# Feed-forward gate and up products as seven block products in place of eight

## The chip, the cores and the metric

The kernel runs on one core of one Trainium2 chip. The metric is the device time of one execution in microseconds, the median of several. The program is one forward pass of a small model on 512 tokens, written engine by engine with semaphores: every engine (PE for matrix products, ACT and DVE for elementwise work, POOL, and SP for issuing transfers) has its own instruction list, which it runs in order.

## The reference, cut to what matters

Two of the layers end in a SwiGLU feed-forward on the normed rows (D = 1024, D_FF = 2816, 512 tokens, fp32):

```
def swiglu(h, w_gu, w_down):
    u = h @ w_gu
    g, v = u[..., :D_FF], u[..., D_FF:]
    return (jax.nn.silu(g) * v) @ w_down

h = h + swiglu(rmsnorm(h, norm_g[layer, 1]), ffn_w_gu[layer], ffn_w_down[layer])
```

All other parts (recurrent mixer, compressed attention, retention and window attention, experts) are not touched.

## The kernel before, in words

Activations lie transposed: features on the 128 partitions, 512 tokens along the row. fp32 products are made of three fp32r products: each operand is split in a rounded high part and the rest (weights: ACT copies a_raw to a_hi, DVE subtracts to a_lo; `high_a`, `low_a`, for the down weights `high_b`, `low_b`), and `three` (L650 to L654) does high x high, high x low, low x high. hn_hi and hn_lo hold the normed input without its 1/rms, which DVE multiplies in later from rn.

A feed-forward stage has 22 panels of w_a (FF_TILES), two to a pair, so 11 pairs. A panel holds 128 gate columns and 128 up columns for all eight blocks of 128 input features (KT = 8). `linear` makes gate and up tiles of 128 x 512 in two PSUM banks (8 blocks x 3 matmuls each), DVE scales the gate (L2407), ACT takes Silu (L1701), DVE scales again (L2409) and multiplies with up (L2412) to hid, ACT and DVE split it (L1703, L2414). After two panels `down` (48 matmuls into banks 4 to 7, in two halves) multiplies with two panels of w_b, and DVE adds each bank to h (`add_y`, L2236). `ffn` runs the first pair apart (`linear_first` follows the input blocks as they come; `sums`, `root_wide` and `inverse_wide` make rn meanwhile) and the other ten in a loop. SP loads w_a panels (1024 KB) and w_b panels (512 KB) with `load_a` and `load_b`, each when the split of the panel two before is done. POOL only helps with the sum of squares. Banks and buffers alternate with the panel's parity; semaphores a_ready, b_ready, tile_ready, tile_free, hid_ready, y_ready and y_free order the engines.

## Time and profile before

| | us |
|---|---|
| runs | 2140.57, 2140.81, 2142.0; median 2140.81 |
| profiled execution, span from first to last instruction | 2139.6 |
| PE busy, share of the span | 2097.5, 98% |
| DVE, ACT, POOL busy | 1267.3, 836.2, 270.8 |
| the two feed-forward stages, first to last matmul, about | 246 to 606 and 1037 to 1398 |

The profiled execution's own time is not recorded beside its span; the median of the runs lies 1.2 us above the span. A row of the timeline gives start and duration of an instruction. Matmuls are pipelined, so their spacing is the difference of two starts, not the duration.

### The profile page before, as it was taken

How to read it: one execution, taken by the hardware profiler on the slowest of the kernel's cores; microseconds unless marked ns; L12 is line 12 of the kernel's file. 1: busy time of each engine (PE TensorE's matmuls, PEld its weight loads, DVE VectorE, ACT ScalarE, POOL GpSimd, SP SyncE). 2: the span in 40 equal slices, each digit the busy share in tenths (PEclk: the TensorE clock that was granted, in tenths of full speed). 3: DMA queues.
4: the chain of work that ended last, by engine and by line, in shares of the span. 5: the costliest groups of instructions: out<-in, count | busy, mean ns of one | idle time of the engine just before them, and what ended most of it. 6: DMA issues, size and time to landing. Idle time of an engine off the chain costs nothing.

```text
span 2139.6 us, 27223 instructions
## 1 busy us (share of the span) xinstructions
PE 2097.5 (98%) x10474; PEld 1579.8 (74%) x10474; DVE 1267.3 (59%) x1704; ACT 836.2 (39%) x1258; POOL 270.8 (13%) x234
## 2 busy tenths in 40 slices
PE   8999999999999999999999999999999999999998
PEld 6787788888878877888888888877778884333346
DVE  7887855554587678875655555488775454000038
ACT  6556522222253444774422222264542232222143
POOL 1334200000010064000100000020000023222220
PEclk9999999999999999999999999999999999999999
DMA  5322322223214352122322222212122158999961
GB/s 202 125 94 74 118 92 105 88 88 117 79 64 147 130 172 79 31 46 90 131 91 99 104 88 88 98 61 78 60 99 98 62 239 321 418 408 401 391 238 60
DMA packets 62622, 298.13 MB, mean 139 GB/s; under 512 B 14080, under 2 KB 14464, under 8 KB 34582
## 3 DMA queue, kind: packets, MB, share of 16 engines
q1 hardware_dynamic: 42560, 261.60, 32.0%
q0 software_dynamic: 19552, 34.55, 5.3%
q8 instruction: 63, 1.03, 0.2%
q10 hardware_dynamic: 416, 0.70, 0.1%
q14 instruction: 31, 0.25, 0.0%
HBM read 326.37 MB, written 22.48 MB: 163 GB/s over the span
## 4 chain that ended last, share of the span: by engine, by line
PE 80%; DVE 8%; DMA 5%; ACT 3%; issue 2%; POOL 1%; POOLq 0%; ACTq 0%; DVEq 0%
PE psum L652 21%; PE psum L654 21%; PE psum L653 21%; PE psum L1413 5%; PE psum L1437 3%; DMA panel<-w_m 3%; PE psum L1102 2%; PE psum L1077 1%; DVE a_lo L2137 1%; DMA over_panel<-w_m,over_row 1%; ACT a_hi L1520 1%; DVE xc L2294 1%; DVE hs L2248 1%; ACT hn_hi L1547 0%; PE psum L1235 0%
## 5 line engine op out<-in xcount | busy, mean ns | idle before, releaser
L652 PE MATMUL psum<-hn_hi,a_hi 128*128 128x512 f32 (+1 forms) x1592 | 628.2, 395 | 1.9 <-DVE a_lo L2126 0.9
L654 PE MATMUL psum<-hn_hi,a_lo 128*128 128x512 f32 (+1 forms) x1592 | 618.5, 389 | 0.0
L653 PE MATMUL psum<-hn_lo,a_hi 128*128 128x512 f32 (+1 forms) x1592 | 618.1, 388 | 0.0
L652 PEld LDWEIGHTS psum<-hn_hi,a_hi 128*128 128x128 f32 (+1 forms) x1592 | 297.0, 187 | 73.5 <-issue 7.8
L653 PEld LDWEIGHTS psum<-hn_lo,a_hi 128*128 128x128 f32 (+1 forms) x1592 | 297.1, 187 | 64.8 <-issue 2.4
L654 PEld LDWEIGHTS psum<-hn_hi,a_lo 128*128 128x128 f32 (+1 forms) x1592 | 297.0, 187 | 64.4
L2137 DVE TENSOR_TENSOR a_lo<-a_raw,a_hi 128x2048 fp32r<-128x2048 f32 (+2 forms) x108 | 247.2, 2289 | 69.6 <-ACT a_hi L1520 69.1
L1520 ACT ACTIVATE a_hi<-a_raw 128x2048 fp32r<-128x2048 f32 (+2 forms) x108 | 201.3, 1866 | 71.2 <-PE psum L654 62.0
L2236 DVE TENSOR_TENSOR h<-h,psum 128x512 f32<-128x512 f32 x176 | 119.4, 686 | 78.4 <-PE psum L654 78.4
L3150 POOL TENSOR_TENSOR sq<-sq 128x512 f32<-128x512 f32 x5 | 7.8, 1555 | 1118.2 <-ACT sq L1533 1118.2
L3072 DVE TENSOR_TENSOR xhid<-xsg,psum 128x256 f32<-128x256 f32 x24 | 10.1, 421 | 232.3 <-ACT xsg L2081 232.3
L1701 ACT ACTIVATE sg<-sg 128x512 f32<-128x512 f32 x44 | 27.8, 632 | 286.2 <-DVE sg L2407 286.2
L652 PE MATMUL psum<-hid_hi,b_hi 128*128 128x512 f32 x352 | 137.3, 390 | 2.1 <-DVE h L2236 2.0
L654 PE MATMUL psum<-hid_hi,b_lo 128*128 128x512 f32 x352 | 137.0, 389 | 0.0
L653 PE MATMUL psum<-hid_lo,b_hi 128*128 128x512 f32 x352 | 136.9, 389 | 0.0
L1413 PE MATMUL psum<-panel,xw 128*64 128x512 f32 x512 | 113.4, 595 | 0.0
L2412 DVE TENSOR_TENSOR hid<-sg,psum 128x512 f32<-128x512 f32 x44 | 30.3, 688 | 113.8 <-PE psum L654 113.7
L1703 ACT ACTIVATE hid_hi<-hid 128x512 fp32r<-128x512 f32 x44 | 27.8, 632 | 177.5 <-DVE hid L2412 177.5
L1527 ACT ACTIVATE b_hi<-b_raw 128x1024 fp32r<-128x1024 f32 x64 | 66.9, 1050 | 65.5 <-PE psum L654 63.2
L1413 PEld LDWEIGHTS psum<-panel,xw 128*64 128x64 f32 x512 | 35.4, 137 | 66.8 <-issue 66.5
L2143 DVE TENSOR_TENSOR b_lo<-b_raw,b_hi 128x1024 fp32r<-128x1024 f32 x64 | 79.7, 1252 | 1.0 <-ACT b_hi L1527 1.0
L652 PEld LDWEIGHTS psum<-hid_hi,b_hi 128*128 128x128 f32 x352 | 66.1, 188 | 17.4 <-issue 2.6
(533 smaller groups left out, 3261.2 us busy)
## 6 DMA issues: line engine op xcount, KB each, us to landing
a_raw<-w_a SPq DMA_DIRECT2D x115, 1024.0 KB, 5.0
panel<-w_m SPq DMA_DIRECT2D x96, 1024.0 KB
b_raw<-w_b SPq DMA_DIRECT2D x64, 512.0 KB, 3.4
q_scratch<-q_hi POOLq DMA_DIRECT2D x7, 384.0 KB
q_scratch<-qb_lo POOLq DMA_DIRECT2D x7, 384.0 KB
q_hi<-q_scratch POOLq DMA_DIRECT2D x7, 384.0 KB
q_lo<-q_scratch POOLq DMA_DIRECT2D x7, 384.0 KB
token_rows<-nat POOLq DMA_DIRECT2D x4, 512.0 KB, 5.5
```

Source lines behind the costliest of these rows:

```text
L652: pe.matmul(out, w_hi, x_hi, start=first, stop=False)
L653: pe.matmul(out, w_hi, x_lo, start=False, stop=False)
L654: return pe.matmul(out, w_lo, x_hi, start=False, stop=last)
L1102: mm = pe.matmul(bank[6 + at % 2][side * DV:(side + 1) * DV, t * P:(t + 1) * P], w, x, start=i == 0, stop=i == len(steps) - 1)
L1413: mm = pe.matmul(bank[v][rows, :], xw[:, v, k, rows], w[half][:, k % 4 * 2 * EFF:(k % 4 + 1) * 2 * EFF], start=k == 0, stop=k == KT - 1)
L1437: mm = pe.matmul(bank[4 + 2 * v + hb][rows, :], xturn[:, v, f * P + half * SLOTS:f * P + (half + 1) * SLOTS], w[half][:, f * D + hb * 512: ...
L1520: act.activation(a_hi[s % 2][:, 0:w], a_raw[s % 2][:, 0:w], ACT.Copy).then_inc(a_rounded, 1)
L1527: act.activation(b_hi[s % 2][:, :], b_raw[s % 2][:, :], ACT.Copy).then_inc(b_rounded, 1)
L2137: V.tensor_tensor(a_lo[s % 2][:, 0:w], a_raw[s % 2][:, 0:w], a_hi[s % 2][:, 0:w], ALU.subtract) \
L2143: V.tensor_tensor(b_lo[s % 2][:, :], b_raw[s % 2][:, :], b_hi[s % 2][:, :], ALU.subtract) \
L2236: V.tensor_tensor(h[:, m, :], h[:, m, :], bank[4 + m % 4][:, :], ALU.add).then_inc(y_free, 1)
L2412: V.tensor_tensor(hid[:, f, :], sg[:, f, :], ps[1][:, :], ALU.mult).then_inc(tile_free, 2)
```

## The change

Both feed-forward stages, panels 3 to 22 of each (NFAST = 20). The gate and up products of a panel are a 2 x 2 by 2 x 2 block product: rows of blocks are gate and up; the sum runs over input features 0 to 511 and 512 to 1023 (A_11 and A_12 for gate, A_21 and A_22 for up); columns are tokens 0 to 255 and 256 to 511. Winograd's form of Strassen's scheme does it with seven products of 4 blocks x 3 matmuls of 256 columns. It needs four sums of weight blocks (S_1 to S_4) per panel and four combinations of the input (T1 to T4) once per stage.

- The host packs a panel as A_11, A_12, A_21, A_22, 512 columns each, with no other change.
- Input combinations: ACT writes the gained input (`gain_x`), POOL combines (`make_tx`), ACT and DVE split (`high_tx`, `low_tx`).
- Weight sums: SP loads A_21 and A_22 into w_sum (`begin_sums`), then POOL issues four transfers that add: `sum_3` (A_11 from DRAM onto w_sum), `sum_2`, `sum_1`, `sum_4` (from SBUF onto SBUF), 256 KB each, each after the one before has landed. S_3 and S_2 are made a panel ahead.
- Split parts go to seven slots (slot_hi, slot_lo) in place of a_hi and a_lo, five ACT copies and five DVE subtractions a panel (one of 1024 elements, the rest of 512).
- PE runs `fast_phase` per panel: P_1, P_2, then P_3 of the panel before, P_6, P_4 of the panel before, P_7, P_5. P_6, P_3, P_5 and P_4 add onto banks that hold earlier products; ACT copies the partial results out between them (`copy_1` to `copy_3`), DVE adds or subtracts them (`add_11`, `add_21`, `add_22`). `down` of a pair now runs between the two phases of the next pair, and the last panel's P_3 and P_4 are `fast_last`.
- SP issues transfers in the order in which buffers come free (`load_fast`), and rel and dk are loaded by POOL after the second stage and no longer before it.

In DVE's `first_pair` the order is low_a, low_tx(0), low_b, inverse_wide, gate(0), low_1, hidden(0), gate(1), low_hid(0), hidden(1), low_tx(1), low_hid(1), low_b, add_11, scale_11, low_tx(2), two add_y, low_tx(3), two add_y, low_s2, low_s3, low_s1, low_1, low_b, four add_y, low_s4, low_a22, low_s2, low_s3, add_22, low_s1. ACT's and DVE's `ffn` call first_pair, fast_b, then fast_a and fast_b in a loop. `used_at`, `split_at`, `summed_at` and the like are counts that the semaphores have before stage g. The core of the diff, its indentation cut:

```diff
+def begin_sums(a, g, i, v):
+    if i > 1:
+        sp.wait_ge(w_summed[v], summed_at(g) + 64 * i - 64)
+        sp.wait_ge(w_split, split_at(g) + 10 * i + 5 * v - 15)
+    sp.dma_start(w_sum[:, v, :, :, :].rearrange("p a k n -> p (a k n)"),
+                 w_a[a + v + 2 * i, :, 2 * S:4 * S]).then_inc(sum_begun[v], 16)
+def load_raw(a, g, i, v):
+    if i > 1:
+        sp.wait_ge(w_split, split_at(g) + 5 * (2 * i + v - 3) + 2)
+    load_a(a + v, i)
+def load_fast(a, b, q, g):
+    sp.wait_ge(hn_ready, KT * (q + 1))
+    for v in range(2):
+        begin_sums(a, g, 1, v)
+        load_raw(a, g, 1, v)
+    load_b(b, 1)
+    for i in range(1, FF_TILES // 2 - 1):
+        begin_sums(a, g, i + 1, 0)
+        load_b(b + 1, i)
+        load_raw(a, g, i + 1, 0)
+        begin_sums(a, g, i + 1, 1)
+        load_b(b, i + 1)
+        load_raw(a, g, i + 1, 1)
+    load_b(b + 1, FF_TILES // 2 - 1)
+    sp.wait_ge(w_split, split_at(g + 1) - 4)
...
+def seven(out, slot, x_hi, x_lo, again=False):
+    for k in range(KT // 2):
+        mm = three(out, slot_hi[:, slot, k, :], slot_lo[:, slot, k, :], x_hi(k), x_lo(k),
+                   not again and k == 0, k == KT // 2 - 1, again)
+    return mm
+def fast_phase(sa, g, i, v, between=None):
+    n, m = sa + v + 2 * i, v - 2 + 2 * i
+    first = isinstance(i, int) and m == 0
+    x, z, y = bank[2 * v][:, 0:HALF], bank[2 * v + 1][:, 0:HALF], bank[2 * v + 1][:, HALF:S]
+    split, copied = split_at(g) + 5 * m, copied_at(g) + 3 * m
+    pe.wait_ge(tile_free, 2 * n - 2)
+    pe.wait_ge(w_split, split + 1)
+    seven(x, P_1, *hn_block(0, slice(0, HALF))).then_inc(w_used, 1)
+    seven(y, P_2, *hn_block(KT // 2, slice(0, HALF))).then_inc(w_used, 1)
+    if not first:
+        pe.wait_ge(part_copied, copied)
+        pe.wait_ge(w_split, split + 2)
+        seven(bank[2 - 2 * v][:, 0:HALF], P_3, *hn_block(KT // 2, slice(HALF, S)), again=True) \
+            .then_inc(w_used, 1)
+    else:
+        between()
+        pe.wait_ge(tx_ready, tx_at(g + 1))
+    pe.wait_ge(part_copied, copied + 1)
+    pe.wait_ge(w_split, split + 3)
+    seven(x, P_6, *tx(T2), again=True).then_inc(w_used, 2 if first else 1)
+    if not first:
+        pe.wait_ge(a_ready, n)
+        pe.wait_ge(part_added, added_at(g) + 2 * m)
+        seven(bank[3 - 2 * v][:, 0:HALF], P_4, *tx(T4), again=True).then_inc(tile_ready, 2)
+    pe.wait_ge(part_added, added_at(g) + 2 * m + 1)
+    pe.wait_ge(w_split, split + 4)
+    seven(z, P_7, *tx(T3)).then_inc(w_used, 1)
+    pe.wait_ge(part_copied, copied + 2)
+    pe.wait_ge(w_split, split + 5)
+    seven(x, P_5, *tx(T1), again=True).then_inc(w_used, 1)
+def fast_last(sa, g):
+    pe.wait_ge(part_copied, copied_at(g + 1))
+    pe.wait_ge(w_split, split_at(g + 1))
+    seven(bank[2][:, 0:HALF], P_3, *hn_block(KT // 2, slice(HALF, S)), again=True).then_inc(w_used, 1)
+    pe.wait_ge(a_ready, sa + FF_TILES)
+    pe.wait_ge(part_added, added_at(g + 1))
+    seven(bank[3][:, 0:HALF], P_4, *tx(T4), again=True).then_inc(tile_ready, 2)
+def ffn(sa, sb_, e, trips, q, t, g):
+    linear_first(sa, q, blocks=True)
     sums(t)
-    linear(sa + 1)
-    down(sb_, e, 0, hid_hi, hid_lo, P)
-    with pe.Fori(1, trips) as i:
-        linear(sa, i)
-        linear(sa + 1, i)
-        down(sb_, e, i, hid_hi, hid_lo, P)
-
-ffn(A_FF0, B_FF0, E_FF0, FF_TILES // 2, N_FFN0, T_FFN0)
+    linear(sa + 1, blocks=True)
+    fast_phase(sa, g, 1, 0, between=lambda: down(sb_, e, 0, hid_hi, hid_lo, P))
+    fast_phase(sa, g, 1, 1)
+    with pe.Fori(2, trips) as i:
+        fast_phase(sa, g, i, 0)
+        down(sb_ - 2, e - 1, i, hid_hi, hid_lo, P)
+        fast_phase(sa, g, i, 1)
+    fast_last(sa, g)
+    down(sb_, e, trips - 1, hid_hi, hid_lo, P)
...
+def gain_x(k, gain):
+    for j in range(2):
+        act.activation(x_of(k)[:, j, :], h[:, k + KT // 2 * j, :], ACT.Copy, scale=gain(k + KT // 2 * j)) \
+           .then_inc(x_gained, 1)
...
+def high_s4(g, i, v):
+    act.wait_ge(w_summed[v], summed_at(g) + 64 * i)
+    act.wait_ge(w_used, used_at(g) + 6 * (v - 2 + 2 * i) + 3)
+    act.activation(slot_hi[:, P_3, :, :], part(v, S_4), ACT.Copy).then_inc(w_rounded, 1)
+def high_a22(sa, i, v):
+    act.wait_ge(tile_ready, 2 * (sa + v + 2 * i))
+    act.activation(slot_hi[:, P_4, :, :], part(v, A_22), ACT.Copy).then_inc(a_rounded, 1)
...
+def high_s1(sa, g, i, v):
+    m = v - 2 + 2 * i
+    act.wait_ge(w_summed[v], summed_at(g) + 64 * i - 16)
+    if isinstance(i, int) and m == 0:
+        act.wait_ge(tile_ready, 2 * sa + 4)
+    else:
+        act.wait_ge(w_used, used_at(g) + 6 * (m - 1) + 6)
+def copy_1(g, i, v):
+    m = v - 2 + 2 * i
+    act.wait_ge(w_used, used_at(g) + 6 * m + 1)
+    if not (isinstance(i, int) and m == 0):
+        act.wait_ge(part_added, added_at(g) + 2 * m - 1)
+    act.activation(pc1[:, :], bank[2 * v][:, 0:HALF], ACT.Copy).then_inc(part_copied, 1)
+def copy_2(sa, g, i, v):
+    act.wait_ge(w_used, used_at(g) + 6 * (v - 2 + 2 * i) + 4)
+    act.wait_ge(tile_free, 2 * (sa + v - 1 + 2 * i))
+    act.activation(pc2[:, v, :], bank[2 * v][:, 0:HALF], ACT.Copy).then_inc(part_copied, 1)
+def copy_3(g, i, v):
+    m = v - 2 + 2 * i
+    act.wait_ge(w_used, used_at(g) + 6 * m + 6)
+    if not (isinstance(i, int) and m == 0):
+        act.wait_ge(part_added, added_at(g) + 2 * m)
+    act.activation(pc3[:, :], bank[2 * v][:, 0:HALF], ACT.Copy).then_inc(part_copied, 1)
+def first_pair(sa, sb_, e, t, g, gain):
+    gain_x(0, gain)
+    high_a(sa + 1)
+    for k in range(1, KT // 2):
+        gain_x(k, gain)
+    high_tx(g, 0)
+    high_b(sb_)
+    root_wide(t)
+    high_b(sb_ + 1)
+    high_1(sa, g, 1, 0)
+    high_tx(g, 1)
+    silu(e, 0, 0)
+    high_tx(g, 2)
+    high_hid(0, tile_free, 2 * sa + 2)
+    silu(e, 0, 1)
+    high_tx(g, 3)
+    high_hid(1, tile_free, 2 * sa + 4)
+    copy_1(g, 1, 0)
+    high_s2(sa, g, 1, 0)
+    high_s3(sa, g, 1, 0)
+    high_s1(sa, g, 1, 0)
+    high_1(sa, g, 1, 1)
+    high_b(sb_, 1)
+    copy_2(sa, g, 1, 0)
+    high_s4(g, 1, 0)
+    high_a22(sa, 1, 0)
+    high_s2(sa, g, 1, 1)
+    high_s3(sa, g, 1, 1)
+    copy_3(g, 1, 0)
+    high_s1(sa, g, 1, 1)
+def fast_a(sa, sb_, e, i, g):
+    copy_1(g, i, 0)
+    high_b(sb_ - 1, i)
+    silu(e, i - 1, 1)
+    copy_2(sa, g, i, 0)
+    high_a22(sa, i, 0)
+    high_hid(1, hid_made, hid_at(g) - 2 + 2 * i)
+    high_1(sa, g, i, 1)
+    high_s4(g, i, 0)
+    copy_3(g, i, 0)
+    high_s2(sa, g, i, 1)
+    high_s3(sa, g, i, 1)
+    high_s1(sa, g, i, 1)
+    high_b(sb_, i)
+def fast_b(sa, e, i, g, last=False):
+    copy_1(g, i, 1)
+    if not last:
+        high_1(sa, g, i + 1, 0)
+    high_s4(g, i, 1)
+    silu(e, i, 0)
+    copy_2(sa, g, i, 1)
+    if not last:
+        high_s2(sa, g, i + 1, 0)
+    high_a22(sa, i, 1)
+    high_hid(0, hid_made, hid_at(g) - 1 + 2 * i)
+    if not last:
+        high_s3(sa, g, i + 1, 0)
+    copy_3(g, i, 1)
+    if not last:
+        high_s1(sa, g, i + 1, 0)
+def ffn(sa, sb_, e, trips, t, g, gain):
+    first_pair(sa, sb_, e, t, g, gain)
+    fast_b(sa, e, 1, g)
+    with act.Fori(2, trips - 1) as i:
+        fast_a(sa, sb_, e, i, g)
+        fast_b(sa, e, i, g)
+    fast_a(sa, sb_, e, trips - 1, g)
+    fast_b(sa, e, trips - 1, g, last=True)
+    high_b(sb_ + 1, trips - 1)
+    act.wait_ge(w_used, used_at(g + 1) - 2)
+    high_a(sa + FF_TILES)
+    silu(e, trips - 1, 1)
+    high_hid(1, hid_made, hid_at(g + 1))
...
+def add_11(g, m, v):
+    V.wait_ge(part_copied, copied_at(g) + 3 * m + 1)
+    V.wait_ge(w_used, used_at(g) + 6 * m + 2)
+    V.tensor_tensor(sg[:, v, 0:HALF], pc1[:, :], bank[2 * v + 1][:, HALF:S], ALU.add).then_inc(part_added, 1)
+def scale_11(g, m, v):
+    V.wait_ge(part_added, added_at(g) + 2 * m + 1)
+    V.tensor_tensor(sg[:, v, 0:HALF], sg[:, v, 0:HALF], rn[:, 0:HALF], ALU.mult)
+def scale_12(used, v):
+    V.wait_ge(w_used, used)
+    V.tensor_tensor(sg[:, v, HALF:S], bank[2 * v][:, 0:HALF], rn[:, HALF:S], ALU.mult).then_inc(gate_scaled, 1)
+def add_21(n, v):
+    V.wait_ge(tile_ready, 2 * n + 2)
+    V.tensor_tensor(up[:, 0:HALF], bank[2 * v + 1][:, 0:HALF], pc2[:, v, :], ALU.subtract).then_inc(tile_free, 2)
+def add_22(g, m, v):
+    V.wait_ge(part_copied, copied_at(g) + 3 * m + 3)
+    V.tensor_tensor(up[:, HALF:S], bank[2 * v + 1][:, 0:HALF], pc3[:, :], ALU.subtract).then_inc(part_added, 1)
+def scale_gate(e, i, v):
+    V.wait_ge(gate_done, 2 * (e - E_FF0 + i) + v + 1)
+    V.tensor_tensor(sg[:, v, :], sg[:, v, :], rn[:, :], ALU.mult).then_inc(gate_scaled, 1)
+def fast_hidden(e, n, i, v):
+    V.wait_ge(gate_scaled, 4 * (e - E_FF0 + i) + 2 * v + 2)
+    V.wait_ge(tile_free, 2 * n + 2)
+    V.tensor_tensor(hid[:, v, :], sg[:, v, :], up[:, :], ALU.mult).then_inc(hid_made, 1)
...
+def fast_a(sa, sb_, e, i, g):
+    n, m = sa + 2 * i, 2 * i - 2
+    add_11(g, m, 0)
+    scale_11(g, m, 0)
+    low_b(sb_ - 1, i)
+    scale_12(used_at(g) + 6 * m + 3, 1)
+    scale_gate(e, i - 1, 1)
+    add_21(n - 1, 1)
+    fast_hidden(e, n - 1, i - 1, 1)
+    low_a22(n, 0)
+    low_hid(e, i - 1, 1)
+    low_1(g, m + 1, 1)
+    low_s4(split_at(g) + 5 * m + 7, 0)
+    add_22(g, m, 0)
+    low_s2(g, m + 1, 1)
+    low_s3(g, m + 1, 1)
+    for k in range(4):
+        add_y(sb_ - 2 + 2 * i, k)
+    low_s1(g, m + 1, 1)
+    low_b(sb_, i)
+    for k in range(4, KT):
+        add_y(sb_ - 2 + 2 * i, k)
+def fast_b(sa, e, i, g, last=False):
+    n, m = sa + 2 * i, 2 * i - 2
+    add_11(g, m + 1, 1)
+    scale_11(g, m + 1, 1)
+    if not last:
+        low_1(g, m + 2, 0)
+    scale_12(used_at(g) + 6 * m + 9, 0)
+    low_s4(split_at(g) + 5 * m + (11 if last else 12), 1)
+    scale_gate(e, i, 0)
+    add_21(n, 0)
+    fast_hidden(e, n, i, 0)
+    if not last:
+        low_s2(g, m + 2, 0)
+    low_a22(n + 1, 1)
+    low_hid(e, i, 0)
+    if not last:
+        low_s3(g, m + 2, 0)
+    add_22(g, m + 1, 1)
...
+    fast_a(sa, sb_, e, trips - 1, g)
+    fast_b(sa, e, trips - 1, g, last=True)
+    low_b(sb_ + 1, trips - 1)
+    low_a(sa + FF_TILES)
+    scale_12(used_at(g + 1), 1)
+    scale_gate(e, trips - 1, 1)
+    add_21(sa + FF_TILES - 1, 1)
+    fast_hidden(e, sa + FF_TILES - 1, trips - 1, 1)
+    low_hid(e, trips - 1, 1)
...
+def make_tx(g, k):
+    x = tx_of(k)
+    pool.wait_ge(x_gained, gained_at(g) + 2 * k + 2)
+    pool.tensor_tensor(x[:, 3, :], x[:, 1, :], x[:, 3, :], ALU.subtract).then_inc(tx_made, 1)
+    pool.tensor_tensor(x[:, 1, :], x[:, 0, :], x[:, 1, :], ALU.subtract).then_inc(tx_made, 1)
+    pool.wait_ge(tx_made, tx_at(g, 4) + 4 * k + 1)
+    pool.tensor_tensor(x[:, 0, :], x[:, 3, :], x[:, 0, :], ALU.subtract).then_inc(tx_made, 1)
+    pool.wait_ge(tx_made, tx_at(g, 4) + 4 * k + 3)
+    pool.tensor_tensor(x[:, 2, :], x[:, 2, :], x[:, 0, :], ALU.add).then_inc(tx_made, 1)
+def sum_3(sa, g, i, v):
+    if i > 1:
+        pool.wait_ge(w_summed[v], summed_at(g) + 64 * i - 64)
+    pool.wait_ge(sum_begun[v], begun_at(g) + 16 * i)
+    pool.dma_start(w_sum[:, v, S_3, :, :].rearrange("p k n -> p (k n)"), w_a[sa + v + 2 * i, :, 0:S],
+                   accum_op=ALU.add).then_inc(w_summed[v], 16)
+def sum_2(g, i, v):
+    pool.wait_ge(w_summed[v], summed_at(g) + 64 * i - 48)
+    pool.dma_start(w_sum[:, v, S_2, :, :], w_sum[:, v, S_3, :, :], accum_op=ALU.add).then_inc(w_summed[v], 16)
+def sum_1(sa, g, i, v):
+    pool.wait_ge(a_loaded[(sa + v) % 2], 16 * ((sa + v) // 2 + i) + 16)
+    pool.wait_ge(w_summed[v], summed_at(g) + 64 * i - 32)
+    pool.dma_start(part(v, S_1), part(v, A_22), accum_op=ALU.add).then_inc(w_summed[v], 16)
+def sum_4(g, i, v):
+    pool.wait_ge(w_summed[v], summed_at(g) + 64 * i - 16)
+    pool.wait_ge(w_split, split_at(g) + 5 * (v - 2 + 2 * i) + 1)
+    pool.dma_start(part(v, S_4), w_sum[:, v, S_2, :, :], accum_op=ALU.add).then_inc(w_summed[v], 16)
+def ffn(sa, g):
+    for k in range(KT // 2):
+        make_tx(g, k)
+    sum_3(sa, g, 1, 0)
+    sum_2(g, 1, 0)
+    sum_1(sa, g, 1, 0)
+    sum_3(sa, g, 1, 1)
+    sum_2(g, 1, 1)
+    sum_4(g, 1, 0)
+    for i in range(1, FF_TILES // 2):
+        more = i + 1 < FF_TILES // 2
+        if more:
+            sum_3(sa, g, i + 1, 0)
+        sum_1(sa, g, i, 1)
+        if more:
+            sum_2(g, i + 1, 0)
+        sum_4(g, i, 1)
+        if more:
+            sum_1(sa, g, i + 1, 0)
+            sum_3(sa, g, i + 1, 1)
+            sum_2(g, i + 1, 1)
+            sum_4(g, i + 1, 0)
...
 n = w.shape[1] // 2
-return _cols(w, [[slice(f * P, (f + 1) * P), slice(n + f * P, n + (f + 1) * P)] for f in range(n // P)])
+panels = _cols(w, [[slice(f * P, (f + 1) * P), slice(n + f * P, n + (f + 1) * P)] for f in range(n // P)])
+return panels.reshape(-1, P, KT, 2, P).transpose(0, 1, 3, 2, 4).reshape(-1, P, WA)
```

## Rows read from the trace of the kernel before

**Rows 1.** The page's busy times (us, share, instructions)
```profile
PE 2097.5 (98%) x10474; PEld 1579.8 (74%) x10474; DVE 1267.3 (59%) x1704; ACT 836.2 (39%) x1258; POOL 270.8 (13%) x234
```

**Rows 2.** Windows: one pair of the second feed-forward stage
```profile
1070.00:1102.66 32.66, 32.66 (x146) 27.06 (x145) 17.68 (x21) 8.15 (x8) 0.00 (x0) 1.00 0.27 97
```

**Rows 3.** Waits of PE from 246 to 612 us: total, times, longest
```profile
PE psum L652 <- DVE h L2236: 0.9, 1, 0.9
```

**Rows 4.** Timeline, PE, 512 columns: start, duration
```profile
300.04 0.39 PE L652 MATMUL psum<-hn_hi,a_hi 128*128 128x512 f32 x1
...
302.53 0.39 PE L654 MATMUL psum<-hn_hi,a_lo 128*128 128x512 f32 x1
302.76 0.39 PE L652 MATMUL psum<-hid_hi,b_hi 128*128 128x512 f32 x1
```

**Rows 5.** Timeline, PE, 256 columns; a new output tile begins at 708.46
```profile
702.94 0.28 PE L654 MATMUL psum<-a_hi,hn_lo 128*128 128x256 f32 x1
...
708.34 0.28 PE L654 MATMUL psum<-a_hi,hn_lo 128*128 128x256 f32 x1
708.46 0.28 PE L652 MATMUL psum<-a_hi,hn_hi 128*128 128x256 f32 x1
```

**Rows 6.** Groups by form: weight loads of these matmuls
```profile
L653 PEld LDWEIGHTS psum<-a_lo,hn_hi 128*128 128x128 f32 x64 | 12.3, 192 | 0.0
```

**Rows 7.** Groups by form, ACT and DVE: busy, mean ns
```profile
L1520 ACT ACTIVATE a_hi<-a_raw 128x2048 fp32r<-128x2048 f32 x101 | 192.1, 1904 | 64.2 <-PE psum L654 55.1 <-DMA a_raw<-w_a 9.2
L1547 ACT ACTIVATE hn_hi<-h,cn 128x512 fp32r<-128x512 f32 x56 | 38.8, 715 | 26.3 <-DVE h L2681 11.4 <-DVE h L2236 5.1 <-PE psum L654 5.0
L1703 ACT ACTIVATE hid_hi<-hid 128x512 fp32r<-128x512 f32 x44 | 27.8, 632 | 177.5 <-DVE hid L2412 177.5
L1507 ACT ACTIVATE a_hi<-a_raw 128x1024 fp32r<-128x1024 f32 x16 | 16.2, 1049 | 29.3 <-PE psum L654 26.8 <-DMA a_raw<-w_a 2.5
L2081 ACT ACTIVATE xsg<-psum 128x256 f32<-128x256 f32 x24 | 9.2, 384 | 139.6 <-PE psum L1413 133.4 <-issue 6.1
L2137 DVE TENSOR_TENSOR a_lo<-a_raw,a_hi 128x2048 fp32r<-128x2048 f32 x101 | 235.3, 2330 | 66.5 <-ACT a_hi L1520 66.0
L2143 DVE TENSOR_TENSOR b_lo<-b_raw,b_hi 128x1024 fp32r<-128x1024 f32 x64 | 79.7, 1252 | 1.0 <-ACT b_hi L1527 1.0
L2412 DVE TENSOR_TENSOR hid<-sg,psum 128x512 f32<-128x512 f32 x44 | 30.3, 688 | 113.8 <-PE psum L654 113.7
L2126 DVE TENSOR_TENSOR a_lo<-a_raw,a_hi 128x1024 fp32r<-128x1024 f32 x16 | 19.0, 1221 | 5.2 <-ACT a_hi L1507 5.0
L3072 DVE TENSOR_TENSOR xhid<-xsg,psum 128x256 f32<-128x256 f32 x24 | 10.1, 421 | 232.3 <-ACT xsg L2081 232.3
```

**Rows 8.** Timeline at both stages' starts: high_a on ACT, down on PE
```profile
248.35 1.90 ACT L1520 ACTIVATE a_hi<-a_raw 128x2048 fp32r<-128x2048 f32 x1
268.91 0.39 PE L652 MATMUL psum<-hid_hi,b_hi 128*128 128x512 f32 x1
...
1042.40 1.91 ACT L1520 ACTIVATE a_hi<-a_raw 128x2048 fp32r<-128x2048 f32 x1
1059.30 0.39 PE L652 MATMUL psum<-hid_hi,b_hi 128*128 128x512 f32 x1
```

**Rows 9.** One line's instructions, POOL: min/median/max ns
```profile
L3150 POOL TENSOR_TENSOR sq<-sq,tmp x10: 1292/1558/3157, 242.4 to 1728.6; 128x512 f32<-128x512 f32 x10
```

**Rows 10.** DMA issues: count, KB each, us to landing
```profile
a_raw<-w_a SPq DMA_DIRECT2D x115, 1024.0 KB, 5.0
b_raw<-w_b SPq DMA_DIRECT2D x64, 512.0 KB, 3.4
dk<-decay POOLq DMA_DIRECT2D x1, 1024.0 KB, 5.2
ptr<-p_t POOLq DMA_DIRECT2D x1, 512.0 KB, 6.9
cs<-rope POOLq DMA_DIRECT2D x1, 256.0 KB, 3.1
```

291 lines of the change are left out of this document (206 added, 85 removed).

## The prediction

> **What bounds the kernel now.** I read the page's busy times first: PE is busy 2097.5 of 2139.6 us [rows 1]. Then the windows of one feed-forward pair: PE 32.66 of 32.66 us with 146 matmuls, DVE 17.68, ACT 8.15, DMA 0.27 of its time [rows 2]. The list of waits has one wait of PE in the whole first feed-forward stage, 0.9 us [rows 3]. So in both stages the end is set by the spacing of matmuls, and everything else has room. The timeline gives that spacing, which is not the 389 ns that a row shows as duration (matmuls overlap): from 300.04 to 302.76 lie 12 matmuls of 512 columns, 0.2267 us each, and the step from one product to the next is no longer [rows 4].
>
> **Term 1, PE.** A panel was 48 matmuls of 512 columns: 48 x 0.2268 = 10.89 us. It becomes 7 products x 4 blocks x 3 = 84 matmuls of 256 columns. The trace has this shape, 128x128 weights under 256 fp32r columns: from 702.94 to 708.34 lie 45 of them, 0.120 us each, and where the next output tile begins, behind a wait that is already met, the step is 0.12 again [rows 5]. A weight load per matmul, 192 ns long in its row but started every 0.12 us, keeps that pace [rows 6]. 84 x 0.120 = 10.08, so 0.81 us less for each of 20 panels in each of two stages: 40 x 0.806 = -32.2 us. The first pair of each stage is unchanged. A pair is then 2 x 10.08 + 10.89 (down) = 31.05 us for 32.66. The Trainium skill ("TensorE: Matmul & The Clock Gate", Back-to-back issue gap) gives a spacing of columns / 2.4 + 2.5 ns: 109 and 216 ns, which would make this term 40 x (10.36 - 9.17) = -48 us. The rows show 13 ns beyond the columns at either width, not 2.5, and they decide.
>
> **Term 2, ACT and DVE inside the loop.** Nearest rows [rows 7]: 1024 elements on ACT 1.05 us, 512 elements 0.63 on ACT and 0.69 on DVE, 256 elements 0.38 and 0.42, DVE b_lo 1.25. For a pair that makes on DVE 10 x 0.42 + 2 x 1.22 + 2 x 1.25 + 24 x 0.69 = 25.7 of 31.05 us (with the eight add_y), and on ACT under 15. Below the bound, but I followed both queues through a phase, since they are in order. In fast_b DVE can first scale at 3.1 us (P_2), is at scale_gate by 6.6, add_21 by 7.4 (P_4 done), and ends low_s1 at 12.6, i.e. 2.5 us into the next phase, where add_11 is due at 3.0. Every copy that PE needs (copy_1 before P_6, copy_2 before P_5, copy_3 before P_3) has 2.9 us or more and ACT needs under 1.5. The thinnest place is down: DVE reaches add_y(0) at 14.4 and finishes at 15.1; PE wants the bank at 10.08 + 5.44 = 15.5. Cost 0; if that 0.4 us of cover is gone, up to 0.5 us a pair, 10 us in all.
>
> **Term 3, the end of each stage.** fast_last puts P_3 and P_4 of the last panel straight behind P_5, with no work between, and down follows. Count from the end of P_5. ACT: copy_3 to 0.6, high_b to 1.65, the next stage's high_a (2048 elements, 1.90) to 3.5. DVE: add_22 to 1.1, low_b to 3.0, low_a (2.33) to 5.9, and only then scale_12 6.4, silu 7.1, scale_gate 7.8, add_21 8.4, fast_hidden 9.1, high_hid 9.8, low_hid 10.6. PE: waits 0.7 for copy_3, P_3 and P_4 to 3.6, the first hidden tile's 12 matmuls of down to 6.3, then waits to 10.7. That is 0.7 + 4.4 = 5.1 us a stage, +10.2. Before, the same place cost nothing [rows 3]. Bounds: 2.5 each, if low_a were not in DVE's way, to 6.5, if high_b and low_b ran only then and add their waits.
>
> **Term 4, the start of each stage.** ACT's gain_x and POOL's make_tx are new. gain_x(0), two rows of 0.72 us like those of hn_hi [rows 7], stands ahead of high_a, which ran at 248.35 and 1042.40 [rows 8], so make_tx starts at 249.8 and 1043.8. (high_a itself has room: its panel is wanted ten us later. root_wide is 2.8 us late in the second stage, behind the gains; the first fast panel needs only the first tile's hid by then, and has it 0.8 us ahead.) It is 16 POOL additions of 256 columns. POOL's row of 512 columns goes from 1.29 to 3.16, median 1.56 [rows 9]; half of it is 0.65 to 1.6 each, and I take 0.8: 12.8 us, ending 262.6 and 1056.6. PE begins the first fast panel where down stood, at 268.91 and 1059.30 [rows 8], so the first sum starts 6.3 and 2.7 us ahead. The adding transfers of the first panels then run one behind another; call the time of one L, from issue to landing. sum_3, sum_2, sum_1 beside the second panel's sum_3, then sum_4 take 4L. begin_sums of the next pair waits for that sum_4 (3.4 [rows 10], with issues 4.0), then come its sum_3 and, one issue later, the second panel's sum_4, which so lands 4.7 + 6L after the start. high_s4 waits for it with silu and copy_2 queued behind on ACT (+1.7), and P_5 of the second fast panel, 26.8 us after the first, waits for copy_2. The stall is 6L - 26.7 us in the first stage and 6L - 23.1 in the second.
>
> **L** is not in the trace: no transfer adds. From below, 256 KB on POOL's queue landed in 3.1 us; from above, 1024 KB in 5.2 and 512 KB once in 6.9 [rows 10]. An adding transfer reads two sides and writes one; if it costs like three times its bytes, 768 KB, it lies two thirds between 3.1 and 5.2: I take 4.5. The stalls are 0.3 and 3.9: +4.2 us. At 3.1 they are 0, at 6.9 they would be 14.7 and 18.3. The Trainium skill ("DMA: Bandwidth & Descriptors", Anatomy of one DMA) fits 2.0 us + bytes / 436 GB/s: 2.6 us for 256 KB, 3.8 for three times that, which would put term 4 at 0. The row for the same size is 3.1, not 2.6.
>
> **The loop of transfers.** Per pair, the landing of sum_4 of one panel frees w_sum for begin_sums, then sum_3, then sum_2 must be issued before POOL reaches the other panel's sum_4: twice round that is 4L + two begin_sums (3.4 alone, 6.6 right behind a 1024 KB load) + 1.4 of issues. At 4.5 it is 29.4 us, under the 31.05 that PE takes, so it costs 0. The SP queue's loads have 4 us and more: a panel may be loaded once S_4 and A_22 of two panels before are split, lands 5.0 us later and is rounded some 9 us after that issue.
>
> **Sum.** -32.2 + 10.2 + 4.2 = -17.8 us, with 0 for the loop. The profiled execution has a span of 2139.6, and the median of the runs is 1.2 above it. 2139.6 - 17.8 = 2121.8, and with the 1.2 around it 2123.
>
> **Rivals.**
> *The transfers become the bound (slower).* The cycle passes 31.05 us at L = 4.9 if both begin_sums stay as above, and at 5.7 once it slides and no load lies ahead of it (3.4 each). From there each us of L adds 4 us to some 9 pairs in 2 stages, 72 us. With the stalls of term 4 it turns the sign at L = 5.75. At 6.5, near the 512 KB row of 6.9, it gives 2141 - 22 (terms 1 and 3) + 28 (term 4) + 58 (0.8 x 72) = 2205. For it: eight adding transfers a pair in a chain, and 6 MB moved in 31 us in all where it was 3 MB. Against: the 256 KB row of 3.1 [rows 10], and DMA at 0.27 of its time [rows 2]. 0.17.
> *No change.* A satisfied wait stands before each of the seven products. At 280 products in all, 0.06 us for each costs 16.8 and leaves the sum at -1.0: 2140; some of it with add_y late in down gives 2137 to 2145. Against: [rows 4, 5] show no gap at such steps. 0.06.
> *The whole saving.* L of 3.8 or less, so no stall at the start, and half of the end's stall: -32.2 + 5.1 gives 2114; with no stall at either place 2109. 0.09.
> *The change doesn't cut PE time.* It does by count unless 256-column matmuls run slower beside twice the traffic; nothing in [rows 5] says so, and I count it in the second rival.
>
> **How the numbers follow.** My forecast, 2115 to 2136, has 0.68: its low end is terms 1 and 3 alone with an end of 3.5 us, its high end L = 5.3 (stalls of 5.1 and 8.7) with 3 us lost at add_y. A measurement of this kernel tells 0.2%, 4.3 us, from no change. Faster: 0.68 + 0.09 = 0.77. Within: 0.06. Slower: 0.17. The range takes the forecast's case, a part of the whole saving from 2111 on, the second rival, and the mild part of the first up to 2155; what lies beyond (most of the first) is about 0.17.
>
> **What would show it.** Step 1: 1680 matmuls of 256 columns per stage, started every 0.12 us inside a product and from one product to the next; a pair takes 31.05 us, PE without idle. Step 2: no PE wait on DVE h in down. Step 3: ahead of the last down of each stage PE waits 4 to 5 us for hid_lo, with a_lo of 2048 elements in DVE's row before scale_12. Step 4: the second fast panel of the second stage waits for ACT's copy, itself behind high_s4 and a DMA. The transfers: landing 4.5 us after issue. The prediction is wrong if they land after more than 5.7 us, if pairs in the middle of the loop take over 31.5 us, or if make_tx takes 20 us and more.

## The result, and the profile after

The changed kernel takes 2180.2 us (median of 4 runs, 2176.3 to 2184.2) where the kernel before takes 2141.3 beside it: ratio 1.0184, 95% interval 1.017 to 1.0199. It is 39 us slower; forecast were 18 us less. The profiled execution has a span of 2176.9 us.

Busy times, mean shares and queues on the page of the changed kernel:
```profile
PE 2082.0 (96%) x11914; PEld 1625.4 (75%) x11914; DVE 1395.5 (64%) x2072; ACT 965.5 (44%) x1602; POOL 444.3 (20%) x426
...
q0 software_dynamic: 42592, 76.50, 16.7%
...
PE 48%; DMA 29%; DVE 9%; issue 7%; POOL 4%; ACT 4%; POOLq 0%; ACTq 0%; DVEq 0%
```
PE is busy 15.5 us less than in [rows 1], not 32, while the time grew: it now waits. And the chain that ended last, which was PE for 80% of the span before, is now PE for 48% and DMA for 29%. A pair of the loop in the windows, and then 210 us of it:
```profile
384.85:417.71 32.86, 31.69 (x217) 29.16 (x216) 23.37 (x38) 13.71 (x24) 6.92 (x8) 1.00 0.76 192
350.00:560.00 210.00, 201.96 (x1355) 185.30 (x1354) 146.39 (x238) 84.60 (x149) 43.30 (x50) 1.00 0.76 193
```
This stands against [rows 2]: this pair takes 32.86 us where a pair took 32.66 and should take 31.05; the DMA engines are busy 0.76 of the time, not 0.27. What PE waits for in the first stage, from 246 to 622 us (total, times, longest), where [rows 3] had one wait of 0.9:
```profile
PE psum L752 <- ACT pc L1918: 8.7, 8, 1.2
PE psum L752 <- ACT pc L1913: 7.2, 1, 7.2
PE psum L752 <- DVE hid_lo L2702: 2.5, 1, 2.5
PE psum L752 <- DVE sg L2735: 2.2, 5, 0.6
PE psum L752 <- DVE h L2528: 1.5, 3, 1.0
PE psum L752 <- ACT pc L1925: 0.5, 1, 0.5
```
Three different things: up to 1.2 us once a pair (copy_2, with add_11's 0.6), one wait of 7.2 at the start (copy_1), one of 2.5 at the end (hid_lo). The DMA issues of the whole kernel (KB each, median us to landing), against [rows 10]:
```profile
w_sum<-w_a SPq DMA_DIRECT2D x40, 512.0 KB, 4.5
w_sum<-w_a POOLq DMA_DIRECT2D x40, 256.0 KB, 4.2
w_sum<-w_sum POOLq DMA_DIRECT2D x40, 256.0 KB, 7.0
a_raw<-a_raw POOLq DMA_DIRECT2D x40, 256.0 KB, 5.7
a_raw<-w_sum POOLq DMA_DIRECT2D x40, 256.0 KB, 3.6
```
The last four are sum_3, sum_2, sum_1 and sum_4; in the loop the view has landings for the second panel of each pair alone, so the 3.6 of sum_4 leaves out the slow one that the chain shows below. The chain of waits over one pair of the loop (start, us, what):
```profile
384.85 4.36 DMA w_sum<-w_a
...
389.77 0.54 POOL w_sum L3614
390.30 5.39 DMA a_raw<-a_raw
...
395.98 3.58 DMA a_raw<-w_sum
...
399.57 4.80 DMA w_sum<-w_a
...
404.93 0.86 POOL w_sum L3614
405.79 3.59 issue
...
409.40 0.54 POOL w_sum L3619
409.93 7.76 DMA a_raw<-w_sum
...
417.71 4.49 DMA w_sum<-w_a
```
Not one compute instruction is in it. It runs from the copy of A_21 and A_22 into w_sum, here called the lent copy (begin_sums), of panel (i+1,0) at 384.85 over POOL's issue of sum_3, sum_1 and sum_4 of panel (i,1), the lent copy of panel (i+1,1), its sum_3 and, behind the issue of its sum_2, sum_4 of panel (i+1,0), to the next lent copy at 417.71. The "3.59 issue" is the rest of sum_3's landing, which sum_2 waits for. POOL issues in program order, so sum_4 of panel (i+1,0), ready long before, stands behind two transfers of another panel, and then takes 7.76 us where the sum_4 of panel (i,1) took 3.58. Both have a sum_2 issued just ahead of them; what only the slow one has beside it is a 1024 KB load of SP, in flight from 407.00 to 415.19:
```profile
394.73 0.86 POOL L3619 DMA_DIRECT2D w_sum<-w_sum  x1 [3.22 <-DMA w_sum<-w_a]
395.98 0.86 POOL L3629 DMA_DIRECT2D a_raw<-w_sum  x1 [0.39 <-DMA a_raw<-a_raw]
...
407.00 0.33 SPq L609 DMA_DIRECT2D a_raw<-w_a  x1
...
409.93 1.20 POOL L3629 DMA_DIRECT2D a_raw<-w_sum  x1
```

**Where the time is.** With the starts of down in the timeline each stage splits in three, against the sum of the prediction's step 1 (25.5 us to the first down, 35.4 to the next, 31.05 a pair, 23.9 to the last, 10.9 for it). The first stage is 376.6 us long for 344.0: 9.4 more at the start (271.42 to 316.23 is 44.8), 18.7 in the loop (316.23 to 607.22 is 291.0 for 272.3), 4.4 at the end (607.22 to 622.53). The second stage in the same way: 13.5, 20.3, 5.7. The eight pairs between the second down and the tenth take 33.1 us in the mean in the first stage and 33.4 in the second, between 31.8 and 33.9 each: the pair shown above is one of the shorter ones. Together 72 us over the bound of PE, 39.0 of them in the loop, 22.9 at the starts, 10.1 at the ends; -32.2 + 72 = +40, and measured are +39.

### The profile page after: what moved, and what is told of

The parts are those of the page before. It is cut to its first block, busy times and chain, and to the rows that moved or that the text cites. A ratio compares the mean times of both kernels' runs of the same rounds, so it can differ in the third digit from the quotient of the medians.

```text
span 2176.9 us, 31992 instructions
## 1 busy us (share of the span) xinstructions
PE 2082.0 (96%) x11914; PEld 1625.4 (75%) x11914; DVE 1395.5 (64%) x2072; ACT 965.5 (44%) x1602; POOL 444.3 (20%) x426
## 4 chain that ended last, share of the span: by engine, by line
PE 48%; DMA 29%; DVE 9%; issue 7%; POOL 4%; ACT 4%; POOLq 0%; ACTq 0%; DVEq 0%
PE psum L752 11%; PE psum L754 11%; PE psum L753 11%; DMA a_raw<-w_sum 10%; DMA w_sum<-w_a 8%; DMA a_raw<-a_raw 5%; PE psum L1568 4%; DMA panel<-w_m 4%; PE psum L1592 3%; PE psum L1257 2%; PE psum L1232 1%; DVE a_lo L2429 1%; POOL w_sum L3614 1%; DMA over_panel<-w_m,over_row 1%; ACT a_hi L1675 1%
## 5 line engine op out<-in xcount | busy, mean ns | idle before, releaser
L752 PE MATMUL psum<-hn_hi,a_hi 128*128 128x512 f32 (+2 forms) x952 | 379.1, 398 | 1.9 <-DVE a_lo L2418 0.9
L754 PE MATMUL psum<-hn_hi,a_lo 128*128 128x512 f32 (+2 forms) x952 | 369.5, 388 | 0.0
L753 PE MATMUL psum<-hn_lo,a_hi 128*128 128x512 f32 (+2 forms) x952 | 369.2, 388 | 0.0
L752 PE MATMUL psum<-tx_hi,slot_hi 128*128 128x256 f32 x640 | 185.9, 291 | 38.5 <-ACT pc L1918 18.1
L2429 DVE TENSOR_TENSOR a_lo<-a_raw,a_hi 128x2048 fp32r<-128x2048 f32 (+3 forms) x68 | 155.8, 2291 | 46.9 <-ACT a_hi L1675 46.3
L753 PE MATMUL psum<-tx_lo,slot_hi 128*128 128x256 f32 x640 | 182.3, 285 | 0.0
L754 PE MATMUL psum<-tx_hi,slot_lo 128*128 128x256 f32 x640 | 182.2, 285 | 0.0
L3501 DVE TENSOR_TENSOR xhid<-xsg,psum 128x256 f32<-128x256 f32 x24 | 10.1, 421 | 233.1 <-ACT xsg L2373 233.1
L752 PE MATMUL psum<-hn_hi,slot_hi 128*128 128x256 f32 x480 | 136.1, 284 | 3.9 <-ACT pc L1925 2.6
L753 PE MATMUL psum<-hn_lo,slot_hi 128*128 128x256 f32 x480 | 135.8, 283 | 0.0
L754 PE MATMUL psum<-hn_hi,slot_lo 128*128 128x256 f32 x480 | 135.8, 283 | 0.0
```

What stands on the lines that cost most here:

```text
L752: pe.matmul(out, w_hi, x_hi, start=first, stop=False, skip_group_check=again)
L753: pe.matmul(out, w_hi, x_lo, start=False, stop=False, skip_group_check=again)
L754: return pe.matmul(out, w_lo, x_hi, start=False, stop=last, skip_group_check=again)
L2429: V.tensor_tensor(a_lo[s % 2][:, 0:w], a_raw[s % 2][:, 0:w], a_hi[s % 2][:, 0:w], ALU.subtract) \
L3501: V.tensor_tensor(xhid[:, v, :], xsg[:, v, :], bank[v][:, EFF:2 * EFF], ALU.mult).then_inc(xhid_done, 1)
```

## The experiments

Each was timed beside the kernel before; "excess" is what the median is above the 2140.7 to 2141.1 of its own runs of before. In diffs, - is the changed kernel.

**e1_sum4_ahead.** One line moved in POOL's ffn.
```diff
                         sum_1(sa, g, i + 1, 0)
+                        sum_4(g, i + 1, 0)
                         sum_3(sa, g, i + 1, 1)
                         sum_2(g, i + 1, 1)
-                        sum_4(g, i + 1, 0)
```


> One line moved: GpSimd issues the last sum of panel (i+1,0), A_12 + S_2, directly behind the sum A_21 + A_22 of that panel, ahead of the two early sums of panel (i+1,1), so that it no longer waits for a lent copy and an adding transfer of another panel, nor shares the queue with the second of them. Theory (the chain of dependent transfers, in GpSimd's program order, sets the pair): the chain over one pair falls to about 4.4 + 0.5 + 5.4 + 0.3 + 3.6 + 1.0 + 5 + 0.3 + 3.6 = 24 us, under TensorE's 31.05, so a pair takes 31.1 to 31.4 us where it took 32.9 to 33.1; 18 pairs give 30 to 36 us back: 2144 to 2150. Rival (the adding transfers are too slow or too many for the queue, in any order): the pair stays at 32.5 or more, 2170 to 2180. Rival (the order of VectorE's and ScalarE's work sets the pair): 32.7 to 33.1, no change.

Measured 2146.2 us (2143.6 to 2149.1), ratio to before 1.0023 (1.0013 to 1.0034): 34 of the 39 us are gone with one line, as the first theory had it. Downs start at 319.22 and, eight pairs later, 570.21: 31.37 us a pair, the single ones between 31.06 and 32.3. The window of the loop, and PE's waits of the first stage:
```profile
350.00:560.00 210.00, 209.02 (x1438) 195.30 (x1437) 157.20 (x254) 91.91 (x159) 47.45 (x55) 1.00 0.81 198
```
```profile
PE psum L752 <- ACT pc L1918: 1.0, 1, 1.0
```
The wait for copy_1 at the start stays, 7.8 us. The DMA engines are busier (0.81) than in the changed kernel (0.76), and the pair is faster: it was not their capacity, but the order. Every sum_4 in this window now lands in 3.3 to 3.6 us, though another sum is in flight beside each of them; a 1024 KB load is for at most 0.9 us. A sum_2 lands in 3.3 us without such a load beside it (5 of them, from 350 to 560 and 1150 to 1370 us) and in 5.1 to 8.8 with one for 1.5 us or more (21); the one issued at 405.67 took 8.5 with no other sum in flight. No run moved the loads alone, so this is read from the traces and not tested. The rivals of a full queue and of VectorE's order are out for the loop.

**e2_small_adds.** Each adding transfer moves 16 of its 512 columns, so the kernel leaves out nearly all of each sum; waits and issues stay. For instance
```diff
-pool.dma_start(w_sum[:, v, S_2, :, :], w_sum[:, v, S_3, :, :], accum_op=ALU.add)
+pool.dma_start(w_sum[:, v, S_2, 0, 0:16], w_sum[:, v, S_3, 0, 0:16], accum_op=ALU.add)
```


> Each of the four adding transfers of a panel moves 16 of its 512 columns; all waits and issues stay. The weight sums are left out but for those columns, so the output is not the reference's. Theory (the time of the transfers sets the pair): each of them lands in 2 to 3 us, and a pair takes TensorE's 31.05 to 31.2 us; with the first sums done sooner 2130 to 2146. Rival (VectorE's and ScalarE's order, or matmuls that cost more than 0.12 us): the pair stays above 32.5 us and the time above 2170.

Measured 2122.3 us (2120.8 to 2123.6), ratio 0.9914 (0.9899 to 0.9929), below the range expected. Every pair takes 31.06 us (downs at 308.35, 339.41, 370.47), and the big wait at the start is 1.2 us. This is what the seven products are worth when no transfer is late: with 256-column matmuls, seven satisfied waits a panel and more small work on ACT and DVE (13.71 and 23.37 us of the pair above, for 8.15 and 17.68 in [rows 2]), PE's count holds.

**e3_plain_copies.** The four transfers of a panel without accum_op=ALU.add: copies of the same size, with the sums left out.
```diff
-pool.dma_start(part(v, S_1), part(v, A_22), accum_op=ALU.add)
+pool.dma_start(part(v, S_1), part(v, A_22))
```


> The same four transfers of 256 KB a panel as plain copies, without the addition: the weight sums are left out. If the adding itself is what makes them slow, each lands in 3.0 to 4.0 us instead of 3.6 to 7.8 and the pair falls to 31.1 to 31.5 us (2140 to 2150). If the waits between them and their place in the queue are what costs, they land within 0.5 us of the adding ones and the pair stays at 32.5 to 33.1 us (2170 to 2180).

Measured 2133.9 us (2129.8 to 2134.6), ratio 0.9964 (0.9951 to 0.9978), 6 us below the range of either reading; a pair takes 31.06 us in the changed kernel's own order. So the adding is the other half of the cause. POOL's queue from 350 to 560 us, of the changed kernel and then of this one (packets, MB, share of 16 engines):
```profile
q0 software_dynamic: 7229, 13.16, 37.3%
```
```profile
q0 software_dynamic: 4400, 14.42, 20.7%
```
An adding transfer takes 37.3 / 13.16 = 2.8% of the engines for each MB, a copy 20.7 / 14.42 = 1.4%: twice the engine time, in 549 packets a MB for 305. In this window sum_3, sum_2, sum_1 and sum_4 land in 4.2, 7.0, 5.7 and 3.5 us, in the median, and the four copies in 3.4, 2.3, 4.7 and 3.0. The first are of one panel of each pair, so the two rows compare only roughly; sum_2 without a 1024 KB load beside it lands in 3.3 us in e1 and in 2.3 as a copy here, with one in 7.6 in the median there and in 2.5 here.

**e4_start_sums.** The first sums issued between the four groups of make_tx:
```diff
-for k in range(KT // 2): make_tx(g, k)
-sum_3(1,0) sum_2(1,0) sum_1(1,0) sum_3(1,1) sum_2(1,1) sum_4(1,0)
+make_tx(0) sum_3(1,0) make_tx(1) sum_2(1,0) sum_3(1,1) make_tx(2)
+sum_1(1,0) sum_2(1,1) make_tx(3) sum_4(1,0)
```


> GpSimd issues the first sums of each stage between the sixteen additions that make the sums of the activations, instead of behind all of them; the rest is as in the changed kernel. Theory (the late first sums cost 7.2 and 7.7 us of waiting for pc, and the halved TensorE clock behind each wait 1.8 more): both waits fall under 1 us and 14 to 19 us are gone, with the pairs of the loop unchanged at 32.9 to 33.1 us: 2161 to 2167. Rival (what sets the start is ScalarE's order: the copy that TensorE waits for stands behind work that is late anyway): the waits keep more than 5 us each, 2174 to 2182. Rival (the issues of transfers delay the activations' sums, which the first panel needs): a new wait on tx of 2 us or more ahead of the first product with them.

Measured 2179.9 us (2177.6 to 2181.3), ratio 1.0181 (1.0167 to 1.0195): no gain, a miss of the theory. The time is in the second reading's range, but the cause is nearer the third: the issues made make_tx late. From 246 to 622 us PE waits, among others, for
```profile
PE psum L752 <- DVE hid_lo L2702: 5.8, 2, 3.4
PE psum L752 <- ACT pc L1913: 3.6, 1, 3.6
```
The 7.2 us became 3.6, and 3.4 came back inside the first down, for hid_lo of the second tile. VectorE had low_tx(1) behind it by then and waited 2.2 us itself for hid_hi; the one that was late is ScalarE, where high_tx(3) stands ahead of high_hid(1) and waited for the last group of make_tx, which POOL had put off behind its issues:
```profile
276.07 1.06 ACT L1851 ACTIVATE tx_hi<-txf 128x1024 fp32r<-128x1024 f32 x1 [4.35 <-POOL txf L3608]
```

**e5_tail.** At the end of a stage the split of the next stage's first tile goes behind the hidden work (ACT; on DVE low_a is taken out in the same way and stands behind the second add_y).
```diff
-                high_a(sa + FF_TILES)
                 silu(e, trips - 1, 1)
                 high_hid(1, hid_made, hid_at(g + 1))
+                high_a(sa + FF_TILES)
```


> Changed kernel, but at the end of each stage the split of the next stage's first weight tile stands behind the last panel's hidden work: on ScalarE behind the rounding of hid, on VectorE behind the second add_y. The wait for hid_lo of 2.5 and 3.8 us, made of 1.9 us of ScalarE's high_a and 1.4 of VectorE's low_a ahead of it on the queues, falls to under 1.0 us in both stages, and with it the halved TensorE clock of the last down product: 6 to 10 us less than the changed kernel, 2170 to 2174. Rival (the split is only moved onto the path: VectorE is the bound of the last product, or the next stage waits for the tile): the time stays within 3 us, 2177 to 2183. The loop is untouched at 32.9 to 33.1 us a pair.

Measured 2173.3 us (2170.9 to 2176.2), ratio 1.0149 (1.0134 to 1.0163): 7 us less than the changed kernel, as expected. The waits for hid_lo, 2.5 and 3.8 us, are 0.6 and 0.6, but those for h near the end grow, to 1.5 at the longest: add_y now has low_a in its way.

**e12_ahead_tail.** e1's line and e5's tail together.

> The order of e1_sum4_ahead (2146.2) and the tail of e5_tail (7 us when run alone), with the start as in the changed kernel: tells how much of e6_ahead_start_tail's 2137.1 came from its start. If the parts add up, 2146.2 - 7 = 2139, and e6's new start was worth only 2 us, so the first sums are held by how many adding transfers there are and not by when they begin. If the start was worth 5 us or more, this kernel takes 2142 to 2146 and the tail gives less behind a loop that is no longer bound by transfers.

Measured 2142.7 us (2141.2 to 2143.8), ratio 1.0006 (0.9997 to 1.0015), excess 1.8. The tail gave 3.5 us here for 7 alone, so the parts don't quite add, as the second reading had it.

**e6_ahead_start_tail.** e12 with a new start: two groups of make_tx first, and sum_1 of the second panel ahead of sum_4 of the first.
```diff
+make_tx(0) make_tx(1) sum_3(1,0) make_tx(2) sum_2(1,0) sum_3(1,1) make_tx(3)
+sum_1(1,0) sum_2(1,1) sum_1(1,1) sum_4(1,0)
```


> Three changes of order at once, nothing of the arithmetic: the last sum ahead of the next panel's early sums (worth 34 us when run alone); the first sums issued from the third of the four groups of activation sums on, and A_21 + A_22 of the second panel ahead of the last sum of the first; the tail of e5_tail. If the three costs are separate, the start waits (7.8 us in each stage, and some 1.8 of halved clock) and the tail's (2.5 and 3.8) go too: 2146 less 17 to 19 less 6 to 10, 2117 to 2126, faster than the kernel before. Rival (the start has a floor: the first sums still land too late, and a wait of 3 us or more stays, as in e4_start_sums where 3.4 us came back ahead of the first down product): 2127 to 2138.

Measured 2137.1 us (2129.7 to 2142.9), ratio 0.9975 (0.9964 to 0.9986): 0.25% under the kernel before, clear of its interval but far inside 2%, and 43 us under the changed one. The runs spread over 13 us. The parts did not add up to 2117 to 2126; this is the upper edge of what was expected from a start with a floor. From 246 to 345 us:
```profile
PE psum L752 <- ACT pc L1918: 4.1, 1, 4.1
PE psum L752 <- DVE h L2528: 1.1, 2, 0.6
```
Over e12 the start gave 5.6 us. What is left: ACT waited 5.4 us for sum_4 of the second panel, with copy_2 behind it on its queue.

**e9_start_both.** e6, with that sum_4(1,1) issued directly behind sum_4(1,0), ahead of the loop.

> The kernel of e6_ahead_start_tail with one more step of order: the last sum of the second panel, A_12 + S_2, is issued ahead of the loop, directly behind that of the first, and no longer behind two early sums of the third panel. In e6 ScalarE waited 5.4 us for it and TensorE 4.1 us behind that, with a lower clock behind the wait. If that order is the cause, the wait goes in both stages with the clock's part: 8 to 12 us under e6, 2125 to 2130. If the start is bound by the number of adding transfers at once, another wait of about the same size takes its place: 2133 to 2139.

Measured 2137.1 us (2133.1 to 2139.8), ratio 0.9979 (0.997 to 0.9988), as e6, so the second reading. From 246 to 345 us PE waits 4.3 for h (3.0 at the longest) and 1.8 for copy_2; what ACT waited for from 296 to 324:
```profile
ACT slot_hi L1897 <- DMA w_sum<-w_sum: 5.9, 2, 5.0
ACT slot_hi L1867 <- DMA a_raw<-w_a: 5.0, 1, 5.0
```
The 4.1 us fell to 1.8, and 3.0 came up at the next down: a sum_2 lands late, high_s2 and low_s2 wait, and add_y stands behind them; ACT waits for a load of w_a itself too. While the panels catch up, the order only says which transfer is late.

**e10_tx_first.** e9 with all of make_tx ahead of the sums again.

> The kernel of e9_start_both, but all sixteen additions for the activation sums stand ahead of the first sums again, as in the changed kernel. If VectorE's queue (the splits of the activation sums ahead of add_y) is what holds the first down product, where e6 still shows waits for h of 1.1 and 4.3 us, they fall under 1 us in both stages, and since the first sums have slack the time is 2 to 5 us under e9. If the first sums have no slack (they start 6 us later), the wait for pc comes back with 4 us or more: 2130 to 2140.

Measured 2148.6 us (2146.4 to 2150.1), ratio 1.0032 (1.002 to 1.0044), above both ranges: the first sums have no slack. The first is issued 7 us later (at 267.45 for 260.21) and the kernel takes 11.5 us more, with waits of 4.2 for pc and 3.9 for h in the first stage.

**e7_pool_adds.** The sums as additions on GpSimd; no lent copies and no adding transfers. For instance
```diff
-pool.dma_start(w_sum[:, v, S_2, :, :], w_sum[:, v, S_3, :, :], accum_op=ALU.add)
+pool.tensor_tensor(w_sum[:, v, S_2, :, :], w_sum[:, v, S_3, :, :], part(v, A_22), ALU.add)
```


> The four sums of a panel are tensor_tensor additions of 512 columns on GpSimd, in place of adding transfers; the lent copies are gone, the transfers go back to those of the kernel before, and the sums are made in the panel that uses them, in order. From the 256-column additions at the start of the stage (0.74 us alone, up to 2.7 beside VectorE): 1.5 us each alone, 6 a panel of 15.5; up to 5.4 each beside VectorE, 21.6 a panel. If nearer the first: the pair is 31.1 to 31.5 us, 2130 to 2150. If VectorE and GpSimd slow each other (from 3.9 us each on) GpSimd is the bound, and VectorE's own work grows too: 2180 to 2300. I take the middle, 2.5 us each, 10 a panel, with VectorE late by some tenths a panel: 2140 to 2165.

Measured 2148.4 us (2145.7 to 2149.6), ratio 1.0032 (1.0022 to 1.0042): 32 us under the changed kernel, near e1, and in the range expected. A pair takes 31.4 us. POOL's groups by form (busy, mean ns):
```profile
L3616 POOL TENSOR_TENSOR w_sum<-w_sum,a_raw 128x512 f32<-128x512 f32 x40 | 72.2, 1806 | 5.7
...
L3621 POOL TENSOR_TENSOR a_raw<-a_raw 128x512 f32<-128x512 f32 x40 | 57.1, 1427 | 6.8 <-POOL w_sum L3616 6.8
```
Four of them, 1.4 to 1.8 us each, are 6.2 us a panel. What it costs is on DVE: from 350 to 560 us the same 512-element subtraction, first in e7 and then in e6:
```profile
L2713 DVE TENSOR_TENSOR slot_lo<-a_raw,slot_hi 128x512 fp32r<-128x512 f32 x14 | 17.3, 1235 | 0.0
```
```profile
L2712 DVE TENSOR_TENSOR slot_lo<-a_raw,slot_hi 128x512 fp32r<-128x512 f32 x13 | 8.9, 684 | 0.0
```
At the start, where DVE has the least room, PE waits 6.5 us for h.

**e8_pool_adds_tail.** e7 with e5's tail.

> The kernel of e7_pool_adds with the tail of e5_tail: 6 to 10 us under e7_pool_adds if the tail's cost is its own; the same within 3 us if not.

Measured 2144.9 us (2141.4 to 2147.2), ratio 1.0018 (1.0009 to 1.0027): 3.4 us, as in e12, and between the two that were expected (6 to 10, or none within 3).

**e11_half_pool.** e6's tail and its start (but for sum_1 of the second panel, which opens the loop); sum_1 and sum_4 on GpSimd as in e7, sum_3 and sum_2 as adding transfers, so that each kind has half.

> The kernel of e6_ahead_start_tail, but the two sums that are written into the loaded panel (A_21 + A_22 and A_12 + S_2) are tensor_tensor additions on GpSimd, of the 1.4 to 1.5 us measured in e7_pool_adds, and only the two early sums stay adding transfers; the sum A_21 + A_22 of a panel stands first on GpSimd's queue. Theory (at the start it is the number of adding transfers at once, a busy share of the DMA engines near 0.8, that holds the panels back, and each keeps its place in the queue): half of them gone, the share falls to about 0.55 and the waits of the second and third panel for pc fall under 1 us; the pair stays at 31.1 to 31.4 us; 2124 to 2131. Rival (VectorE at the start is the bound: with GpSimd's additions beside it add_y is later still, as in e7_pool_adds with its waits of 6.5 us for h): 2135 to 2148.

Measured 2135.2 us (2132.5 to 2139.0), ratio 0.9976 (0.9966 to 0.9985). From 270 to 350 us the DMA engines are busy 0.55 of the time, for 0.78 in e6, as the theory had it, and the loop keeps its 31.06 us; but the rival was right on the time. From 246 to 345 us PE waits 3.3 us for h, 3.0 at the longest, and 2.1 for pc. Halving the adding transfers left waits of 5 us here, of DVE and of transfers, and no run took both away. Which of DVE and the transfers is worth more there is open. With e6 and e9 this is the third order that ends at 2135 to 2137, which no run separates.

## Why the prediction was wrong

**Term 1 was right,** in mechanism and size. From 302.80 to 303.99 (timeline in the last section) ten steps of 256 columns take 0.119 us each; e2, e3 and e6 have pairs of 31.06 us for the 31.05 worked out. The seven products save their 32 us. With the transfers all but gone, e2 takes 2122.3 us, where the sum of the terms said 2123.

**Term 2 was right,** cost 0: in e2's loop PE waits for neither DVE nor ACT. The waits for add_11 and copy_2 in the changed kernel's loop are of instructions that stand behind a late sum on their queues, and go with it (e1).

**Term 3 was right:** 10.1 us for both ends, 10.2 predicted. high_a and low_a stand where the step put them, as DVE's timeline of the first stage shows:
```profile
606.56 1.76 DVE L2429 TENSOR_TENSOR a_lo<-a_raw,a_hi 128x1536 fp32r<-128x1536 f32 x1
608.23 0.42 DVE L2743 TENSOR_TENSOR sg<-psum,rn 128x256 f32<-128x256 f32 x1
```
The waits themselves are shorter than 4.4 (2.5, where the tile is of 1536 elements and not 2048, and 3.8). The slower clock behind them, below, for which the prediction had no price, makes up for it: the queues were read rightly, but that the sizes agree to 0.1 us is in part luck. e5 took 7 us of it back.

**Term 4 failed in size, 22.9 us for 4.2.** Two of its parts. make_tx was taken at 16 x 0.8 = 12.8 us; it took 17.8 (249.39 to 267.14), with rows between 0.73 and 2.67 us:
```profile
252.51 2.67 POOL L3608 TENSOR_TENSOR txf<-txf 128x256 f32<-128x256 f32 x1
...
267.14 1.11 POOL L3614 DMA_DIRECT2D w_sum<-w_a  x1
```
And L. The formula 6L - 26.7 at L = 5.3, with sums begun 4.5 us later, gives 9.6 us; seen were a wait of 7.2 and some 1.6 of clock. It named sum_4 and copy_2; the wait that came first was the one behind sum_1 of the same panel (copy_1), which POOL issues only behind a sum_3 of the next pair. That the first sums have no slack is shown by e10. e6 brings the starts (first down to next) to 42.3 us in both stages, from 44.8 and 47.4; no order that makes the sums came below 41.7 (e9, where the next pair is longer for it), and e2, where they are not made, had 37 and 38, still above 35.4.

**"The loop of transfers" is the step that turned the sign,** 39.0 us for 0. What it counts was right: four landings, two lent copies and the issues. What failed is L, the landing of an adding transfer, and less so the issues. In the pair shown, the landings are 5.39, 3.58, 4.45 (404.93 to 409.38) and 7.76: mean 5.3, not 4.5; the lent copies 9.2, not 10.0; the issues some 2.5 (rows of 0.5 to 0.9 us), not 1.4. 21.2 + 9.2 + 2.5 = 32.9, the period, for the 29.4 predicted: 3.2 us more by the landings, 1.1 by the issues, 0.8 less by the lent copies. This is the rival "the transfers become the bound", which had 0.17: it was to decide from L = 4.9 on with lent copies of 10.0 in all, or from 5.7 with 3.4 each, and turn the sign at 5.75. The forecast's high end, L = 5.3, still had the loop at 0, by the second of these; but the lent copies did not come down to 3.4 (4.36 and 4.80), and with 9.2 and 2.5 the period passes 31.05 already at a mean landing of (31.05 - 9.2 - 2.5) / 4 = 4.8. By its own sign, landings of more than 5.7 us, the mean of 5.3 would not have marked the prediction wrong; its other sign, pairs of over 31.5 us, did. The pair shown is 1.8 us over 31.05, the sixteen pairs of both stages 2.2 in the mean, 35 of the 39 us; the other 4 lie ahead of the last downs (25.9 and 25.8 us for 23.9). In the five pairs from 384.85 to 549.78 us the chain of waits is of transfers and their issues alone, 31.9 to 33.9 us each.

Why L was too small: the row of 256 KB [rows 10] was a copy landing alone. An adding transfer takes twice the engine time of a copy (e3), and it lands in 3.3 to 3.6 us where no 1024 KB load is in flight beside it, but in 7.8 (sum_4) and 7.0 in the median (sum_2) where one is. A single number L for all of them had hidden what the order does to each: the prediction named the place (sum_2 must be issued before POOL reaches the other panel's sum_4) and priced the issue there, but not that sum_4 then falls beside SP's load. It saw such a neighbour for the lent copy alone: the 6.6 us right behind a load is shown by no row, and the nearest one, in e1 at 405.35, took 8.5. Both causes are needed: with e1's order sum_2, sum_1 and sum_3 are as slow (7.5, 6.1 and 4.9 us in the loop) and only sum_4 is out of their way and the load's (3.3), and the pair is PE's again; with e3's copies it is PE's in the old order.

**The whole.** Starts +22.9, loop +39.0, ends +10.1, PE -32.2: +39.8 for +39 measured. The estimate of 2205 at L = 6.5 was of the right kind; the low chance came from the 3.1 us of a lone copy in [rows 10] and from the busy share of 0.27 in [rows 2], which says nothing of a chain that has one transfer in flight at a time.

## What to carry to other kernels

A chain of dependent transfers has a period of its own: write it out once round (landings, issues, and every transfer that an in-order queue puts in between), and give each landing its own price from what else is in flight then, the loads of other queues included, not one for all. Where it comes within a tenth of the bound, order the issues by what they free next: the line that moved was worth 34 us, more than the arithmetic saved. A busy share of DMA is no evidence for or against it; the faster kernel had the higher share.

## What the runs showed of the hardware

**The clock can halve behind a wait of PE.** Behind the wait of 7.24 us the matmuls of 256 columns start every 0.214 us, and then every 0.12 again (timeline):
```profile
298.49 0.58 PE L752 MATMUL psum<-tx_hi,slot_hi 128*128 128x256 f32 x1 [7.24 <-ACT pc L1913]
298.87 0.41 PE L753 MATMUL psum<-tx_lo,slot_hi 128*128 128x256 f32 x1
...
302.50 0.35 PE L752 MATMUL psum<-tx_hi,slot_hi 128*128 128x256 f32 x1
...
302.80 0.28 PE L754 MATMUL psum<-tx_hi,slot_lo 128*128 128x256 f32 x1
...
303.99 0.28 PE L752 MATMUL psum<-tx_hi,slot_hi 128*128 128x256 f32 x1
```
17 steps in 3.63 us where 2.04 are usual: 1.6 us on top of the wait. That is the lower of the two levels, 1.2 GHz for 2.4; the granted clock of 270 to 300 us is 0.93. The same behind the 2.48 us at the end of the stage (512 columns every 0.43 us from 613.55 to 616.11, granted clock 0.94 from 600 to 630). Behind the 1.2 us waits of the loop it did not fall (1.00). Between these it went either way: in e9 it fell behind 1.83 us (granted clock 0.84 from 295 to 306), and in e3 it stayed at 1.00 behind 2.49 us at the same place of the stage:
```profile
591.48 0.50 PE L752 MATMUL psum<-hid_hi,b_hi 128*128 128x512 f32 x1 [2.49 <-DVE hid_lo L2702]
```
So the length of the one wait does not decide it. The prediction had no price for this. The Trainium skill ("TensorE: Matmul & The Clock Gate", What's actually happening) has TensorE at its lower level once it has been idle and at the upper once it is busy again; the rows of the changed kernel agree, and the one of e3 shows an idle time without the fall.

**GpSimd and VectorE stretch each other.** Beside GpSimd's additions VectorE's subtraction of two SBUF operands went from 684 ns in the mean to 1065 to 1235 in three of a panel's places (e6 and e7), while its add_y, with one operand in PSUM, stayed at 676 for 686. The same line of e7, without and with an addition of GpSimd beside it:
```profile
402.17 0.68 DVE L2713 TENSOR_TENSOR slot_lo<-a_raw,slot_hi 128x512 fp32r<-128x512 f32 x1
410.97 1.54 POOL L3621 TENSOR_TENSOR a_raw<-a_raw 128x512 f32<-128x512 f32 x1 [0.17 <-POOL w_sum L3616]
411.28 1.79 DVE L2713 TENSOR_TENSOR slot_lo<-a_raw,slot_hi 128x512 fp32r<-128x512 f32 x1
```
It goes the other way too: GpSimd's own 256-column additions take 0.73 to 2.67 us, its 512-column ones 1.27 to 2.12. The one of 2.67 began at 252.51, while VectorE's a_lo, with two SBUF operands, ran from 251.75 to 254.58, and ended at 255.18. The Trainium skill ("SBUF — State Buffer", Who interferes with whom) says that a VectorE instruction with two SBUF inputs contends with a GpSimd instruction that reads SBUF, and that one with at most one SBUF input, outside certain fast modes, does not; the trace agrees on both. Term 4's 0.8 us an addition had left it out.

**An adding transfer is cut finer than a copy** (549 packets a MB for 305) and takes twice the engine time for each MB. With 8 KB in place of 256 KB (e2) the median landings, from issue on, are 2.0 to 3.7 us.
